# Six high/low weight slots for the experts, split two steps ahead, and half of the residual's transposes moved under the preceding product

## The reference, cut to what matters

```python
y = jax.nn.sigmoid(gate_dn) * y_dn + jax.nn.sigmoid(gate_sgu) * y_sgu
mix = jnp.einsum("bld,de->ble", y, w_out)
h = layer_norm(DEEPNORM_ALPHA * h + mix, ln1_g, ln1_b)
# router: best of 4 groups, then the best 2 of its 4 experts -> combine
g = jax.nn.silu(jnp.einsum("td,edf->tef", t, expert_w_gate)) \
    * jnp.einsum("td,edf->tef", t, expert_w_up)
g = g * combine[:, :, None]
y = jnp.einsum("tef,efd->td", g, expert_w_down)
h = layer_norm(DEEPNORM_ALPHA * h + y, ln2_g, ln2_b)
```

## Time and profile before

| what | us |
|---|---|
| median of 3 runs | 2995.59 (2990.28 to 2996.71) |
| the profiled execution, its own time | 2997.38 |
| its span (first to last instruction) | 2995.5 |
| of it, from the first expert matmul to the last evacuation | 2650.3 to 2976.7 |

### The profile page before, as it was taken

The page is one execution under the profiler, slowest core; times in us unless marked ns, Lnnn a source line. Parts: engine busy times, 40 slices in busy tenths (PEclk is TensorE's granted clock), DMA queues, the critical chain, the costliest instruction groups (busy, mean ns, idle before and its releaser), DMA issues. The chain is left out here.

```text
span 2995.5 us, 35985 instructions
## 1 busy us (share of the span) xinstructions
PE 2662.7 (89%) x14316; PEld 2238.9 (75%) x14316; DVE 1201.3 (40%) x1657; ACT 700.2 (23%) x1130; POOL 1573.3 (53%) x479
## 2 busy tenths in 40 slices
PE   5999999978999979997999979989899998658785
PEld 3888888866898848775888857879878977646564
DVE  4112011235774632076111243544231446448884
ACT  3111000113212411002100014334310111146563
POOL 2443555442642137764777755644367765145655
PEclk7999999988998999998999989989999999779998
DMA  5443221123220022231222233200032225167773
GB/s 232 201 178 135 67 70 66 49 96 137 70 71 32 1 100 88 96 113 56 94 92 102 79 115 121 93 9 1 1 135 104 94 90 199 51 254 302 266 292 122
DMA packets 52301, 334.96 MB, mean 112 GB/s; under 512 B 6500, under 2 KB 7524, under 8 KB 19344
## 3 DMA queue, kind: packets, MB, share of 16 engines
q1 hardware_dynamic: 50592, 327.44, 29.9%
q0 software_dynamic: 1584, 5.78, 0.5%
HBM read 314.84 MB, written 22.07 MB: 112 GB/s over the span
## 5 line engine op out<-in xcount | busy, mean ns | idle before, releaser
L160 POOL TENSOR_TENSOR whi<-raw,one_col 128x2048 fp32r<-128x2048 f32 (+2 forms) x160 | 533.7, 3336 | 952.7 <-PE bank L180 716.1
L163 POOL TENSOR_TENSOR wlo<-raw,whi 128x2048 fp32r<-128x2048 f32 (+2 forms) x160 | 707.9, 4425 | 12.6
L178 PE MATMUL bank<-uh_a,whi 128*128 128x512 f32 (+1 forms) x704 | 239.0, 339 | 14.8 <-DVE ul_a L600 14.8
L179 PE MATMUL bank<-ul_a,whi 128*128 128x512 f32 (+1 forms) x704 | 237.5, 337 | 0.0
L180 PE MATMUL bank<-uh_a,wlo 128*128 128x512 f32 (+1 forms) x704 | 237.1, 337 | 0.0
L3032 POOL TENSOR_TENSOR moe_wl<-moe_raw,moe_wh 128x2048 fp32r<-128x2048 f32 x30 | 138.8, 4635 | 136.8 <-ACT moe_wh L3139 136.6
L3200 DVE TENSOR_TENSOR moe_wl<-moe_raw,moe_wh 128x2048 fp32r<-128x2048 f32 x54 | 181.6, 3365 | 27.0 <-ACT moe_wh L3139 26.9
L3139 ACT ACTIVATE moe_wh<-moe_raw 128x2048 fp32r<-128x2048 f32 x84 | 160.5, 1913 | 59.1 <-PE bank L3088 30.8
L178 PEld LDWEIGHTS bank<-uh_a,whi 128*128 128x128 f32 x704 | 134.0, 190 | 34.4 <-issue 17.0
L178 PE MATMUL bank<-uh_b,whi 128*128 128x512 f32 x352 | 137.9, 392 | 7.6 <-DVE ul_b L600 6.6
L180 PEld LDWEIGHTS bank<-uh_a,wlo 128*128 128x128 f32 x704 | 134.0, 190 | 14.2
(11 more groups left out here) (552 smaller groups left out, 6539.6 us busy)
## 6 DMA issues: line engine op xcount, KB each, us to landing
moe_raw<-moe_w_dram SPq DMA_DIRECT2D x84, 1024.0 KB, 6.1
cond_ring<-w_ada_dram SPq DMA_DIRECT2D x27, 1024.0 KB, 7.0
raw<-gu_a_dram SPq DMA_DIRECT2D x22, 1024.0 KB, 5.1
raw<-gu_b_dram SPq DMA_DIRECT2D x22, 1024.0 KB, 4.9
raw<-wqkv_dram SPq DMA_DIRECT2D x12, 1024.0 KB, 4.8
raw<-dn_a_dram SPq DMA_DIRECT2D x16, 704.0 KB, 4.1
raw<-dn_b_dram SPq DMA_DIRECT2D x16, 704.0 KB, 4.0
ada_w<-w_ada_dram SPq DMA_DIRECT2D x9, 1024.0 KB, 20.1
```

The lines of the kernel that those rows point to most:

```text
L160: e.nc.gpsimd.tensor_tensor(e.whi[p][:, 0:f], e.raw[p][:, 0:f], e.one_col[:, 0:1].to_broadcast([P, f]), ALU.mult).then_inc(e.w_hi, 1)
L163: e.nc.gpsimd.tensor_tensor(e.wlo[p][:, 0:f], e.raw[p][:, 0:f], e.whi[p][:, 0:f].bitcast(F32), ALU.subtract).then_inc(e.w_split, 1)
L178: e.nc.tensor.matmul(out, wh, xh, start=first, stop=False)
L179: e.nc.tensor.matmul(out, wh, xl, start=False, stop=False)
```

## The change

The change has two parts.

1. **Experts.** `wh` and `wl` get 6 slots each instead of 4. Slots 4 and 5 lie on memory that earlier data leave late (the residual `X`, the token rows `tok`), so `hi(4)` waits for the last row and `hi(5)` for the scatter. ACT, DVE and POOL now treat A and B of step x+2 and D of step x+1 in loop x, where it was A and B of x+1 and D of x. In DVE's list `gate(x)` comes behind `lo` of A(x+2), and `x_lo` behind `gate` of the block's last step. POOL also takes the B tile of each block's last step and no less of the D tiles: 37 low parts instead of 30, DVE 47 instead of 54. The XB loads stay in front of slot 10's load, the load of `LNP` moves from slot 10 to slot 12.
2. **Residual.** The first four groups of residual transposes go in front of `w_sgu`'s last slot on PE, their copies in front of that slot's `y2h` on ACT. For this `w_sgu` is written straight, without a loop.

```diff
-RING_RAW, RING_W = 6, 4
+RING_RAW, RING_W = 6, 6
...
+    def pe_body(pe, p, i, ready):
+        if pe_last is not None and i == last_slot:
+            pe_last(pe)
+        return pe_feature_major(e, p, KT, 2, xh, xl, False, ready=ready)
...
+    def pe_residual(self, pe, n):
+
+        e, t, half = self.e, n // 2, n % 2
+        if n >= 4:
+            pe.wait_ge(self.res_rows, n - 3)
+        else:
+            pe.wait_ge(self.res_in, 16)
+        for k in range(4):
+            last = e.nc.tensor.transpose(e.bank[4 + n % 4][:, k * P:(k + 1) * P],
+                                         self.XR[:, 4 * half + k, t * P:(t + 1) * P], e.ident[:, :])
+        last.then_inc(self.res_turned, 1)
...
-        pe.wait_ge(self.res_in, 16)
-        for n in range(2 * NCH):
-            residual(n)
+        for n in range(4, 2 * NCH):
+            self.pe_residual(pe, n)
...
-    w_at = [BASE + r * 8192 for r in range(6)] + [MAIN, MAIN + 8192]
+    w_at = [BASE, BASE + 16384, BASE + 32768, MAIN, MAIN + 114944, MAIN + 81920]
...
-    by_pool = [s in (2, 3) or key[0] == "D" for s, key in enumerate(order)]
+    by_pool = [s in (2, 3) or key[0] == "D" or (key[0] == "B" and key[1] % EPG == EPG - 1)
+               for s, key in enumerate(order)]
...
-            for x in range(NSTEP):
-                if slot["D", x] >= RING_W:
-                    lo(slot["D", x])
+            for x in range(NSTEP + 1):
                 if x % EPG == 2 and x > EPG:
                     deliver(x // EPG - 1)
+                for key in (("B", x + 2), ("D", x + 1)):
+                    if key in slot and by_pool[slot[key]] and slot[key] > pool_lo[2]:
+                        lo(slot[key])
...
+            act.wait_ge(late.row_ready, NCH)
+            hi(4)
             x_hi(0)
+            act.wait_ge(scattered, 16 * NCH)
+            hi(5)
             for x in range(NSTEP + 1):
                 if x:
-                    silu(x - 1)
-                if x + 1 < NSTEP and slot["A", x + 1] >= RING_W:
-                    hi(slot["A", x + 1])
-                if x:
                     hidden(x - 1)
...
+                if 0 < x < NSTEP - 2:
+                    hi(slot["A", x + 2])
+                if x < NSTEP:
+                    silu(x)
+                if x + 2 < NSTEP:
+                    hi(slot["B", x + 2])
                 if x % EPG == 1 and x > EPG:
                     root(x // EPG - 1)
                 if x % EPG == EPG - 1 and x // EPG + 1 < NBLK:
                     x_hi(x // EPG + 1)
+                if x + 1 < NSTEP:
+                    hi(slot["D", x + 1])
...
             x_lo(0)
+            lo(5)
             for x in range(NSTEP + 1):
                 if x:
-                    gate(x - 1)
-                if x + 1 < NSTEP and slot["A", x + 1] >= RING_W:
-                    lo(slot["A", x + 1])
-                if x:
                     hidden_lo(x - 1)
-                if x + 1 < NSTEP and slot["B", x + 1] >= RING_W:
-                    lo(slot["B", x + 1])
+                if 0 < x < NSTEP - 2:
+                    lo(slot["A", x + 2])
+                if x < NSTEP:
+                    gate(x)
+                if x % EPG == 0 and x:
+                    evacuate(x // EPG - 1)
+                if x + 2 < NSTEP and not by_pool[slot["B", x + 2]]:
+                    lo(slot["B", x + 2])
```

More of the change, by code:

```diff
@@ L1633, in product_gate, with product_gate_split @@
                    dve_body=dve_body, dve_start=dve_start, ready=ready)
-def product_gate_split(e, seg, xh, xl, gate, other, yh, yl, ready=None):
+def product_gate_split(e, seg, xh, xl, gate, other, yh, yl, ready=None, pe_last=None, act_last=None):
     st = Stage(e, seg + "_s")
@@ L1646, in dve_start @@
         dve.wait_ge(e.acc_free, START[seg][0])
+    last_slot = START[seg][1] - START[seg][0] - 1
     def act_body(act, i, p, g):
+        if act_last is not None and i == last_slot:
+            act_last(act)
         act.wait_ge(v_ready, 1 + i)
@@ L1666, in dve_body @@
         last.then_inc(lo_ready, 1)
-    run = Product(seg, lambda pe, p, i, ready: pe_feature_major(e, p, KT, 2, xh, xl, False, ready=ready),
-                  act_body=act_body, dve_body=dve_body, dve_start=dve_start, ready=ready, stages=(st,))
+    def pe_body(pe, p, i, ready):
+        if pe_last is not None and i == last_slot:
+            pe_last(pe)
+        return pe_feature_major(e, p, KT, 2, xh, xl, False, ready=ready)
+    run = Product(seg, pe_body, act_body=act_body, dve_body=dve_body, dve_start=dve_start, ready=ready, stages=(st,),
+                  straight=pe_last is not None)
     return run, lambda eng, k: eng.wait_ge(lo_ready, k // 2 + 1)
@@ L2548, with __init__ @@
 class OutRows:
-    def __init__(self, e, yh, yl, ready, X, XR, LN1, at):
-        self.e, self.st, self.yh, self.yl, self.ready = e, Stage(e, "late"), yh, yl, ready
+    def __init__(self, e, yh, yl, X, XR, LN1, at):
+        self.e, self.st, self.yh, self.yl, self.ready = e, Stage(e, "late"), yh, yl, None
         self.X, self.XR, self.LN1 = X, XR, LN1
@@ L2588, in sp_second, with act_residual, pe_first, act_first @@
         sp.dma_start(self.LN1[:, :], self.e.dram["ln1_rows"]).then_inc(self.ln_in, 16)
+    def pe_residual(self, pe, n):
[8 more added lines that the diff above has]
+        last.then_inc(self.res_turned, 1)
+    def act_residual(self, act, n):
+        t, half = n // 2, n % 2
+        act.wait_ge(self.res_turned, n + 1)
+        self.e.nc.scalar.activation(self.X[:, t, half * 512:(half + 1) * 512], self.e.bank[4 + n % 4][:, :], ACT.Copy,
+                                    scale=ALPHA).then_inc(self.res_rows, 1)
+    def pe_first(self, pe):
+        for n in range(4):
+            self.pe_residual(pe, n)
+    def act_first(self, act):
+        for n in range(4):
+            self.act_residual(act, n)
     def pe(self, pe):
         nc, e = self.e.nc, self.e
[L2593 to L2600, removed]
         def product(p, t, k):
@@ L2977, in moe @@
     slot = {key: s for s, key in enumerate(order)}
-    by_pool = [s in (2, 3) or key[0] == "D" for s, key in enumerate(order)]
+    by_pool = [s in (2, 3) or key[0] == "D" or (key[0] == "B" and key[1] % EPG == EPG - 1)
+               for s, key in enumerate(order)]
+    pool_lo = [s for s, pooled in enumerate(by_pool) if pooled]
     def lo_ready(eng, s):
@@ L3168, in _ @@
             act.wait_ge(e.slot_done, late.b)
-            for s in range(RING_W):
+            for s in range(4):
                 hi(s)
```

26 lines of the change are left out of this document (11 added, 15 removed).

## The result

The changed kernel takes 3039.4 us (median of 4 runs, 3036.09 to 3041.21) where the kernel before takes 2996.15 (4 runs, 2990.28 to 3003.17). The ratio is 1.0141 [1.0122, 1.0160]: 43 us slower. The prediction was 3020, with 3003 to 3036 for the forecast itself: the direction was right, the time lies 3.4 us above the range.

The account below looks back on a forecast made before the run. The prediction took the port shared by DVE and POOL as the bound. 2997.4 - 5 (residual) + 29.5 (experts) = 3021.9, less 1.8 from profiled execution to median, gave 3020 us, range 3003 to 3036.

Parts of the forecast that it names:

- The bound: Experts: the port shared by DVE and POOL, 90% full, 42.9 us of load in a block of 47.9.
- Fourth step: Block's last step: `x_lo` behind low A, `gate` and low B; PE, ready at 39.1, starts A at 49.7 to 54.3.
- Second step: Block's second step: PE loses 6.5 us at `hidden_lo` if DVE gets in, 9.0 at `gate` if POOL keeps the port.
- a POOL low part ready at that moment keeps the port: Experts: a POOL low part ready when the preceding one ends goes before a waiting DVE instruction; read from four blocks.
- Blocks 1 to 5: Experts: a block takes 49.7 to 54.3 us, taken as 52 against 47.9, so +20.5 for the five.
- upper walk: One block walked through its four steps with POOL keeping the port: 54.3 us.
- fair walk: The same block walked with the port changing hands at 43.4: 49.7 us.
- Block 0: Experts' first block: its step 3 turn comes +7.3 to +13 us later; +8 taken.
- Last block: Experts' last block: one more POOL low part and no following rows, +1 us.
- Residual: Front: PE's 12.57 us wait falls to 7 or less, `w_out2`'s first slot ends at about 2533, -5 us, carrying through.
- fair port: Rival for the experts: the port changes hands fairly and late instructions hide, no change, about 2992 us; chance 0.25.
- deep ring: Rival for the experts: both engines always find ready high parts, 1 us a block unused, 2979 us; chance 0.13.

Follow-up runs that it names:

- experiment 11: Kernel before plus the residual part, with POOL's indirect DMA of a delivery placed behind the next low part: 2979.27 us, ratio 0.9942.
- experiment 4: Changed kernel with `x_hi` and `x_lo` of the next block moved up, directly behind `hidden` and `hidden_lo`: 2999.51 us, ratio 1.0018.
- experiment 9: Changed kernel with POOL's indirect DMA placed behind the next low part: 3010.86 us, ratio 1.0049.
- experiment 5: Changed kernel with each POOL low part also waiting for the end of the one before it, a short pause: 3016.85 us, ratio 1.0068.
- experiment 12: Changed kernel with next block's rows directly behind the hidden rows, POOL's share as before, indirect DMA behind the next low part: 2992.27 us, ratio 0.9986.
- pair 6 and 10: 6: changed kernel, next block's rows early, pause between POOL low parts, 2984.96 us. 10: kernel before, residual part, pause between POOL low parts, 2980.34 us.
- experiments 8: Kernel before with POOL's indirect DMA of a delivery placed behind the next low part: 2980.62 us, ratio 0.9940.
- experiment 1: Changed kernel without its residual part, all eight groups of residual turns behind `w_sgu` again: 3040.42 us, ratio 1.0145.

## Why the prediction was right in direction and short in size

- **The bound.** Right for the best kernels: experiment 11 takes 43.4 us for a block against a port load of 42.9. In the changed kernel it is the order on the port that sets the time, not the load: a block takes 54.8 against 45.2.
- **Fourth step, `x_lo` behind `gate` and low B.** Right, the main cause: walked at 12.4 us, measured 14.29, and experiment 4 gives 40 us back.
- **Second step.** The step of the reasoning that failed is the rule read from the earlier trace rows, "a POOL low part ready at that moment keeps the port". It held only directly behind the indirect DMA. In the second step `centre` and DVE's low part went in between (4.53, 6.35), PE lost 1.6 and not 6.5 or 9.0, and `gate` was not late. The four waits of before are all pairs behind that DMA; I had seen the pair and not what stood in front of it.
- **The term that was mis-sized.** Blocks 1 to 5 were taken at +20.5 and measured +34.3. I had walked a block of 49.7 with the port changing hands and 54.3 without, and taken 52, where 54.8 was measured. In the fourth step the pair stands behind the DMA, so DVE lost 11.70 in front of `x_lo`, as in the upper walk.
- **Luck in the upper walk.** That 54.3 and 54.8 agree is partly chance. The walk had 19 to 21 us of waits and so 33 to 35 of PE's work, at full clock. Block 2 had 17.2 of waits (14.3 and two of 1.3 to 1.6) and 37.65 of work, with a granted clock of 0.88 over the block, of 1.00 before the wait of 14.29 and of 0.79 behind it:

```profile
2766.99:2821.80 54.81, 37.65 (x161) 29.73 (x160) 46.97 (x25) 28.91 (x25) 38.13 (x8) 0.88 0.67 249
```

The waits of the second step were overrated and PE's work underrated (the kernel before already had 39.15 of it in its block 2, not "about 35"). The nearness of experiment 9's 49.3 to the fair walk's 49.7 has the same two errors in it.

- **Block 0.** +8 taken, +10.9 measured, inside its bounds.
- **Last block.** +1 taken, -5.3 measured. The runs with six slots have 32 to 37 us there, those with four 39 to 40. I think that without rows to come the ring's lead is free; no run tests it.
- **Residual.** -5 taken, -1.4 measured. The wait fell to 6.8 as predicted (7 or less) and the last `y2l` came 0.9 late (1.4 forecast), but the slot ended 1.3 later than I had it (-3.7), since PE ran at half clock there (last section), and another 3.0 were lost in `w_out2`'s slots 3 and 4, where I had "it carries through". 0.8 came back in the router; that stretch is not steady (59.7 to 61.8 us in the ten profiles with the residual part, 60.7 to 61.8 in the four without), so up to the end of `w_out2` the part is worth 0.7 in every profile, and the 1.5 is not firm.
- **Start.** 5.6 us of drift in untouched code, in the profiled run; no walk could give it. The sum of 3021.9 and the profiled execution's 3041.2 differ by 19.3: 13.8 of the blocks, 2.9 of block 0, -6.3 of the last, 3.6 of the front, 5.6 of drift and -0.3 at the end.
- **The rivals.** The fair port's 2992 took it that late rows hide if the port is fair; experiments 5 (3016.9) and 9 (3010.9) show they don't. The prediction tested it against the Trainium skill ("SBUF — State Buffer", section "SBUF: two separate sides"), by which whichever of the two starts first has the pair for the whole instruction. Read as first come, first served, that fits the second step (`centre` from 2777.70 in front of POOL's part) and the three POOL parts of experiment 9; it fails behind the DMA, where DVE waited from 2798.03 and two POOL parts, the first from 2798.62 on, still went first. The deep ring (2979): with the orders mended six slots were still 13 us slower than four (experiment 12), 5 in the pair 6 and 10.

## What to carry to other kernels

A deeper ring brought nothing here, where the engine that fills it also makes something that PE needs sooner: in an in-order list each step of distance puts more early work in front of late work. When distance grows, check for every small instruction on the way to PE what now stands ahead of it. And where two engines share a port, look at what stands directly in front of a run of the second engine's instructions; moving one DMA by one place took 14.5 us off the kernel before.

## What the hardware showed that I had not expected

- **The port behind an indirect DMA.** A DVE low part that comes to wait while POOL's indirect DMA runs is passed over by each POOL low part that follows without a pause: 11.70 us for two (2798.03), 7.34 for one (2741.70, experiment 12), against 2.27 where none was ready (2787.84). One that comes during the first POOL low part behind the DMA is passed over by the second (9.77, the kernel before). With the short pause behind each POOL low part DVE loses to one alone (7.26 in experiment 5), and with the DMA one place later no DVE low part takes over 6.4 us in experiments 8, 9 and 11. How the DMA leaves the port in that state is not shown; a plain DMA wasn't tried.
- **The clock takes back part of a removed wait.** In the kernel before PE was idle for 12.57 us, ran at half clock for 4.3 us and then at 1.00 to the end of `w_out2`'s first slot. In the changed kernel it turned the residual at 1.00 behind its wait of 0.81, but behind the wait of 3.43 it ran at 0.50 for 10.2 us, with some 26 of the last 60 matmuls in them 0.21 us apart instead of 0.12. The changed kernel, then the one before:

```profile
2525.30:2535.50 10.20, 7.62 (x37) 7.33 (x36) 4.21 (x8) 3.40 (x7) 0.00 (x0) 0.50 0.83 300
```

```profile
2526.60:2537.90 11.30, 11.30 (x97) 11.30 (x96) 0.43 (x1) 0.35 (x2) 0.00 (x1) 1.00 1.12 357
```

Its slots 3 and 4 then take longer at a lower clock with the same matmuls and no waits. With half of the residual's turns in front of `w_sgu`'s last slot (changed kernel), and with all behind it (experiment 1):

```profile
2556.30:2578.00 21.70, 21.70 (x163) 21.70 (x162) 4.25 (x11) 1.26 (x2) 8.14 (x2) 0.84 0.19 77
2578.00:2594.50 16.50, 16.49 (x128) 16.28 (x126) 4.21 (x10) 1.27 (x2) 0.00 (x0) 0.90 0.00 1
```

```profile
2560.00:2580.10 20.10, 20.10 (x162) 20.10 (x161) 4.18 (x10) 1.27 (x2) 8.13 (x2) 0.92 0.05 18
2580.10:2595.20 15.10, 15.02 (x128) 14.81 (x126) 4.27 (x11) 1.27 (x2) 0.00 (x0) 1.00 0.00 1
```

0.84 and 0.90 against 0.92 and 1.00 of full speed (means over the two levels, 1.2 and 2.4 GHz): 3.0 us, most of the 3.7 gained. All ten profiles with the residual part show the longer slots (21.6 and 16.5 us), all four without it the shorter (20.1 and 15.05). So the residual part does it; that it does it through the new pattern of waits is argued, since no run put only the idle time back.
